# A hybrid encoder layer on one core: DeltaNet's inverse in 64x64 tiles, a convolution spread over two rounds, and the experts' products in four column tiles of 32 tokens

## The reference, cut to what matters

```python
# DeltaNet: short convolution, then a chunked delta rule; each chunk solves a
# unit lower triangular system A (here with chunks of 128 tokens)
qkv = silu(centred_depthwise_conv(qkv, conv_w))       # 5 taps
L = where(strict, einsum('bnhid,bnhjd->bnhij', kb, k) * decay, 0.0)
sol = triangular_solve(L + eye, rhs, lower=True, unit_diagonal=True)
# experts: 16, each takes its C = 2*T/16 best tokens (32 prompt + 64 sample = 96)
gates, idx = top_k(softmax(xt @ w_router).T, C)
xe = xt[idx]
h = silu(xe @ w_gate[e]) * (xe @ w_up[e])             # 2048 -> 1024
ye = (h @ w_down[e]) * gates                          # 1024 -> 2048
out = zeros_like(xt).at[idx].add(ye)
```

## Time and profile before

| | us |
|---|---|
| median of 3 runs | 3360.66 (3359.61 to 3364.0) |
| the profiled execution's own time | 3364.69 |
| its span in the trace | 3362.9 |
| DeltaNet, about | 624 to 1640 |
| output projection and routing, about | 1640 to 1990 |
| experts | 1990 to the end |

### The profile page before, as it was taken

How to read it: one execution, slowest core, us unless ns; L and a number is a source line. 1 busy time by engine, 2 the same in 40 slices (tenths; PEclk the granted TensorE clock), 3 DMA queues, 4 the chain that set the end, 5 groups by cost and what they waited for, 6 DMA issues and landing times. The chain is left out here.

```text
span 3362.9 us, 28930 instructions
## 1 busy us (share of the span) xinstructions
PE 3262.4 (97%) x11412; PEld 1742.5 (52%) x11412; DVE 889.7 (26%) x1519; ACT 517.8 (15%) x1349; POOL 381.8 (11%) x400
## 2 busy tenths in 40 slices
PE   8999999999999999989999989999999999999998
PEld 4544555567867767757544643333333333333333
DVE  2001454326546547567301230000000000000000
ACT  4101554122132132041100110000000000000000
POOL 0000100032141141152000000000000000000000
PEclk9999999999999999989999889999999999999999
DMA  4111100211111111040421378888888888888884
GB/s 168 50 67 59 38 26 19 83 51 51 47 35 51 48 35 51 23 150 14 159 104 50 126 281 318 316 317 316 317 316 316 317 316 317 316 317 317 317 308 142
DMA packets 165417, 560.59 MB, mean 167 GB/s; under 512 B 11888, under 2 KB 44488, under 8 KB 143304
## 3 DMA queue, kind: packets, MB, share of 16 engines
q1 hardware_dynamic: 161223, 534.07, 44.0%
q0 software_dynamic: 4096, 25.17, 3.4%
HBM read 524.25 MB, written 34.96 MB: 166 GB/s over the span
## 5 line engine op out<-in xcount | busy, mean ns | idle before, releaser
L2360 PE MATMUL psum<-wbuf,xeT 128*96 128x512 f32 x1040 | 454.1, 595 | 2.1 <-ACT h L2411 1.4
L2360 PE MATMUL psum<-xT,xeT 128*96 128x512 f32 x1008 | 437.6, 592 | 0.0
L1219 PE MATMUL psum<-xT,wbuf 128*128 128x512 f32 x720 | 330.6, 594 | 0.3 <-PEq L611 0.3
L2360 PEld LDWEIGHTS psum<-wbuf,xeT 128*96 128x96 f32 x1040 | 170.1, 164 | 280.0 <-issue 279.0
L2360 PEld LDWEIGHTS psum<-xT,xeT 128*96 128x96 f32 x1008 | 164.3, 163 | 268.3 <-issue 268.3
L1963 PE MATMUL psum<-wbuf,xT 128*128 128x512 f32 x656 | 289.9, 604 | 1.0 <-PEq L1144 1.0
L459 PE MATMUL psum<-wbuf,xT 128*128 128x512 f32 (+1 forms) x704 | 281.1, 559 | 0.9 <-DVE xT L379 0.9
L2378 PE MATMUL psum<-xT,hT 128*96 128x512 f32 x528 | 229.3, 592 | 0.7 <-ACT hT L2406 0.7
L2436 DVE COPY hT<-psum 128x384 f32<-128x384 f32 x16 | 8.9, 557 | 822.6 <-PE psum L2342 822.6
L2378 PE MATMUL psum<-wbuf,hT 128*96 128x512 f32 x496 | 215.5, 592 | 0.7 <-DVE hT L2436 0.7
L1963 PEld LDWEIGHTS psum<-wbuf,xT 128*128 128x128 f32 x656 | 127.1, 195 | 158.7 <-issue 158.7
(11 more groups left out here) (297 smaller groups left out, 3045.4 us busy)
## 6 DMA issues: line engine op xcount, KB each, us to landing
wbuf<-in_w_up SPq DMA_DIRECT2D x47, 2048.0 KB, 9.3
xT<-in_w_gate SPq DMA_DIRECT2D x46, 2048.0 KB, 7.2
xT<-in_w_down SPq DMA_DIRECT2D x33, 2048.0 KB, 9.8
wbuf<-in_w_down SPq DMA_DIRECT2D x31, 2048.0 KB, 8.0
wbuf<-in_w_gate SPq DMA_DIRECT2D x18, 2048.0 KB, 7.3
xT<-in_w_up SPq DMA_DIRECT2D x17, 2048.0 KB, 11.6
wbuf<-in_w_in SPq DMA_DIRECT2D x14, 2048.0 KB, 8.8
wbuf<-in_w_o SPq DMA_DIRECT2D x6, 4096.0 KB, 14.7
```

The source lines that it names most:

```text
L1219: last = nc.tensor.matmul(ps[:, b, 0:SS_], wg[:, m % 2, d, h * P:(h + 1) * P], k.xT[:, d, SP_:T], start=(d == 0), stop=(d == KD - 1))
L2360: last = nc.tensor.matmul(ps[0:CT, 2 * (u // 4) + half, :], xeT[:, q, :], m[:, kk, 512 * half:512 * half + 512], start=(q == 0), stop=(q = ...
```

## The change: what it does, and the diff

In `deltanet`: (1) at levels 1 to 5 `product` and `update` compute only the two 64x64 diagonal blocks, each with a product of its own on rows and columns 0 to 63 or 64 to 127 of the array; `advance` becomes two instructions, one for each block. (2) Of head 1's five taps, two stay behind round 0 and three move to levels 1 to 3 of round 1. (3) The sums of squares come later within the next pair's first projection; those of the last pair move into the projection before it, the last pair's ScalarE order is changed to suit, and its transposes of k come ahead of `gram`.

In `moe`: (4) the 96 tokens are split into G = 3 groups of 32 and the output columns into J = 4 quarters. A product has 32 tokens as stationary columns and writes 32 partitions of PSUM; four products, one for each quarter of the columns, go to the four column tiles of the array: 3 x 4 products where there were 4 of `up` (or 32 x 3 where there were 32 of `down`), each 512 columns long. (5) A unit of weights holds two rows of gate and of up together, or two full row blocks of down; it is loaded by two DMAs of 1 MB in pieces of 8 KB. `up` waits for VectorE's multiply of the expert before, where its gate half waited for SiLU alone. (6) The hidden layer and the result now lie as 4 quarters x 32 tokens on 128 partitions: SiLU and multiply are one instruction each, the hidden layer is transposed by six 128x128 transposes instead of eight, the result is scaled by three instructions after the last unit of `down`. (7) The scatter is three DMAs of 128 quarter rows of 2 KB, and the row numbers and gates are spread over the partitions once, at the start of the stage, by five small VectorE instructions, six transposes and two copies; the routing stage loses a transpose and a copy.

```diff
+                def blockwise(x, n, left, right, lv):
+                    for lo, hi in ((0, P),) if lv == LV else ((0, P // 2), (P // 2, P)):
+                        last = nc.tensor.matmul(ps[lo:hi, x, n * P + lo:n * P + hi], left[lo:hi, x, n, lo:hi], right[lo:hi, x, n, lo:hi],
+                                                start=True, stop=True)
+                    return last
                 def product(i, r, x, lv):
                     pe.wait_ge(s_t[x], i * 18 + 6 * r + lv)
                     if r == 0 and lv == 1:
                         pe.wait_ge(s_kvc, i * 6 + 3)
                     for n in range(4):
-                        last = nc.tensor.matmul(ps[:, x, n * P:(n + 1) * P], lt[:, x, n], tinv[:, x, n], start=True, stop=True)
+                        last = blockwise(x, n, lt, tinv, lv)
                     last.then_inc(s_m1[x], 1)
                 def update(i, r, x, lv):
                     pe.wait_ge(s_p1[x], i * 18 + 6 * r + lv)
                     for n in range(4):
-                        last = nc.tensor.matmul(ps[:, x, n * P:(n + 1) * P], p1[:, x, n], tt[:, x, n], start=True, stop=True)
+                        last = blockwise(x, n, p1, tt, lv)
...
-                        project(i + 1, 0, between={2: lambda: sum_squares(i, 0), 3: lambda: sum_squares(i, 1),
-                                                   6: lambda: sum_squares(i, 2), 8: lambda: sum_squares(i, 3)})
-                        project(i + 1, 1, between={0: lambda: gram(i, 0), 8: lambda: k_transposes(i)})
+                        project(i + 1, 0, between={6: lambda: sum_squares(i, 0), 7: lambda: sum_squares(i, 1),
+                                                   11: lambda: sum_squares(i, 2), 13: lambda: sum_squares(i, 3)})
+                        project(i + 1, 1, between={4: lambda: gram(i, 0), 10: lambda: k_transposes(i)})
                     else:
-                        for n in range(4):
-                            sum_squares(i, n)
+                        k_transposes(i)
...
+                        steps = {6: lambda: output(i)}
+                        if i + 2 == HP:
+                            steps.update({14: lambda: sum_squares(i + 1, 0), 15: lambda: sum_squares(i + 1, 1),
+                                          26: lambda: sum_squares(i + 1, 2), 31: lambda: sum_squares(i + 1, 3)})
+                        project(i + 1, 5, between=steps)
...
-                    copy_tile(i, 5)
+                    if more:
+                        copy_tile(i, 5)
                     square(i, 2)
-                    square(i, 3)
+                    if more:
+                        square(i, 3)
                     act.preload_act_table_set(TABLES)
-                    for n in range(4):
-                        rms(i, n)
+                    rms(i, 0)
+                    if not more:
+                        square(i, 3)
+                    rms(i, 1)
+                    if not more:
+                        copy_tile(i, 5)
+                    rms(i, 2)
+                    rms(i, 3)
...
-                    flat = tt[:, x].rearrange("p n c -> p (n c)")
-                    nc.vector.tensor_tensor(flat, flat, ps[:, x, :], ALU.subtract).then_inc(s_tt[x], 1)
+                    bank = ps[:, x, :].rearrange("p (n c) -> p n c", n=4)
+                    for lo, hi in ((0, P),) if lv == LV else ((0, P // 2), (P // 2, P)):
+                        o = tt[lo:hi, x, :, lo:hi]
+                        last = nc.vector.tensor_tensor(o, o, bank[lo:hi, :, lo:hi], ALU.subtract)
+                    last.then_inc(s_tt[x], 1)
...
+                            if r == 1 and lv <= 3 and more:
+                                convolve(i + 1, 1, [lv + 1])
...
-                            convolve(i + 1, 1)
+                            convolve(i + 1, 1, range(2))
...
+    G, J = CT // 32, 4
+    XBANK = (3, 4, 6, 7)
...
+        h = sb("h", [P, G, FF // J])
         hT = sb("hT", [P, FF // P, CT])
-        ye = sb("ye", [CT, D])
-        gate = sb("gate", [CT, 1])
-        ss = sb("scatter_sample", [CS, 1], U32)
-        sp = sb("scatter_prompt", [CP, 1], U32)
+        ye = sb("ye", [P, G, D // J])
+        gate = sb("gate", [P, G])
+        gates = sb("gates", [P, G, NE])
+        quarter = sb("quarter_rows", [P, G, NE], U32)
+        sq = sb("scatter_rows", [P, G], U32)
+        rep = sb("replicated", [NE, 2, G, J, 32])
...
+                        for x, d in enumerate((gate_d, up_d)):
+                            src = d[bass.ds(ex, 1), :, 2 * u:2 * u + 2, :].rearrange("o p k f -> (o p) (k f)")
+                            sync.dma_start(ring[w % RING][:, 2 * FF * x:2 * FF * x + 2 * FF], src).then_inc(s_w[w % RING], 16)
...
-                        src = down_d[bass.ds(ex, 1), :, :, 512 * q:512 * q + 512].rearrange("o p k f -> (o p) k f")
-                        sync.dma_start(ring[w % RING].rearrange("p (k n) -> p k n", k=8), src).then_inc(s_w[w % RING], 16)
+                        for x in range(2):
+                            src = down_d[bass.ds(ex, 1), :, 2 * q + x, :].rearrange("o p n -> (o p) n")
+                            sync.dma_start(ring[w % RING][:, D * x:D * x + D], src).then_inc(s_w[w % RING], 16)
...
-                        for j in range(4):
-                            f = 4 * b + j
-                            last = nc.tensor.transpose(ps[:, 6 + b, j * CT:(j + 1) * CT], h[:, f * P:(f + 1) * P], k.ident[0:CT, 0:CT])
+                        for g in range(G):
+                            last = nc.tensor.transpose(ps[:, 6 + b, g * P:(g + 1) * P], h[:, g, b * P:(b + 1) * P], k.ident)
...
-                                pe.wait_ge(s_sg, ex)
-                        if u == 4 and w0:
-                            pe.wait_ge(s_h, ex)
+                                pe.wait_ge(s_h, ex)
                         pe.wait_ge(s_w[w % RING], loaded(e, w))
-                        m = ring[w % RING].rearrange("p (k f) -> p k f", k=4)
-                        for kk in range(4):
-                            q = 4 * (u % 4) + kk
-                            for half in range(2):
-                                last = nc.tensor.matmul(ps[0:CT, 2 * (u // 4) + half, :], xeT[:, q, :], m[:, kk, 512 * half:512 * half + 512],
-                                                        start=(q == 0), stop=(q == KD - 1))
+                        m = ring[w % RING].rearrange("p (x k f) -> p x k f", x=2, k=2)
+                        for kk in range(2):
+                            q = 2 * u + kk
+                            for g in range(G):
+                                for j in range(J):
+                                    last = nc.tensor.matmul(ps[32 * j:32 * j + 32, g, :].rearrange("p (x n) -> p x n", x=2),
+                                                            xeT[:, q, 32 * g:32 * g + 32], m[:, :, kk, 256 * j:256 * j + 256],
+                                                            start=(q == 0), stop=(q == KD - 1))
                         last.then_inc(s_u, 1)
                 def down(ex, e, w0, more):
                     pe.wait_ge(s_ha, ex + 1)
                     pe.wait_ge(s_hd, ex + 1)
-                    for q in range(4):
-                        w = w0 + q
-                        if q < 2 and more:
-                            pe.wait_ge((s_xa, s_xd)[q], ex * 2 + 5)
-                        elif q < 2:
-                            pe.wait_ge(s_ye, ex * 4 + 4)
-                        else:
-                            pe.wait_ge(s_ye, ex * 4 + q + 3)
+                    for u in range(4):
+                        w = w0 + u
                         pe.wait_ge(s_w[w % RING], loaded(e, w))
-                        m = ring[w % RING].rearrange("p (k n) -> p k n", k=8)
-                        for f in range(8):
-                            last = nc.tensor.matmul(ps[0:CT, 4 + q % 2, :], hT[:, f, :], m[:, f, :], start=(f == 0), stop=(f == 7))
+                        m = ring[w % RING].rearrange("p (k n) -> p k n", k=2)
+                        for kk in range(2):
+                            f = 2 * u + kk
+                            for g in range(G):
+                                if f == 0 and more and g < 2:
+                                    pe.wait_ge((s_xa, s_xd)[g], ex * 2 + 5)
+                                elif f == 0 and not more:
+                                    pe.wait_ge(s_ye, ex * G + g + 1)
+                                for j in range(J):
+                                    last = nc.tensor.matmul(ps[32 * j:32 * j + 32, 3 + g, :], hT[:, f, 32 * g:32 * g + 32],
+                                                            m[:, kk, 512 * j:512 * j + 512], start=(f == 0), stop=(f == 7))
...
+                pe.wait_ge(s_gc, 1)
+                for which in range(2):
+                    for g in range(G):
+                        last = nc.tensor.transpose(ps[:, 0, (which * G + g) * NE:(which * G + g + 1) * NE],
```

(28 more changed lines are left out.)

81 lines of the change are left out of this document (42 added, 39 removed).

## The result

| | before | after |
|---|---|---|
| median of the runs shown, us | 3360.66 | 3074.22 (3 runs, 3072.95 to 3075.09) |
| ratio to before, 95% interval | | 0.9144 [0.9126, 0.9161] |
| span of the profiled execution, us | 3362.9 | 3071.2 |
| first product of the inverse (line 1289) starts | 774.7 | 771.7 |
| last `product` instruction of the inverse starts | 1612.4 | 1591.5 |

Forecast were 3063 us, with a range of 2995 to 3235 and 0.85 for faster. The measured time is 11 us above the forecast and inside the range. By stages, the experts gave 271.6 us (1373.0 to 1101.4; 258 forecast) and DeltaNet about 18 (837.7 us from the first to the last `product` instruction of the inverse, then 819.8; 40 forecast). The remaining 3 us lie ahead of DeltaNet, where nothing was changed.

The account below looks back on a forecast made before the run. TensorE was taken as the bound, by the columns it streams, with DMA next. From the profiled 3364.7 us, less 258 (experts) and 40 (DeltaNet), came 3067, or 3063 as that execution was 4.0 above the median; range 2995 to 3235.

Parts of the forecast that it names:

- The round of four: Experts' `up` and `down`: four column tiles stream at once, 0.429 us a round, 61.8 us an expert in 144 rounds.
- rival B: Experts' products: a column tile's loads cannot run beside other tiles' products; 0.821 us a round, about 3894 us; chance 9%.
- C: Experts' products: tiles go one after the other, 1.716 us a round, 249 us an expert, near 6000 us; chance 5%.
- TensorE's floor: Experts' stage: TensorE's time for products and transposes, 63.8 us an expert.
- The DMA limit: Experts' stage: DMA becomes the limit; 25 us at 359 GB/s, the rest at 417, 1.5 us added: 69 us an expert.
- Rival A: Experts' stage: full DMA queues hold 343 GB/s throughout, 77.8 us an expert, about 3203 us in all; chance 16%.
- The stage: Experts' stage as a whole: 16 x 69 us with start, loads ahead and tail, 1115 us for 1373, -258 us.
- the last unit behind its landing: End of the experts' stage: 5 us added for the last unit of weights behind its landing.
- Levels: DeltaNet levels 1 to 5: 64x64 blocks take 0.5 us off each of 60 levels, -30 us.
- The halves: DeltaNet's `advance` in two instructions: 2 x 0.412 for 0.675 us, +0.3 us a level for both x.
- The spread convolution: DeltaNet, three pairs: TensorE's 2.30 us wait goes, -7 us; taps in round 1 charged 5; net -2 us.
- The last pair's start: DeltaNet's last pair: sums and first two norms within the projection take 8 us off the 26.0 us start.

Follow-up runs that it names:

- Half the bytes: Changed kernel with each DMA of weights in the experts' stage bringing half its bytes, stale data in the rest, every product kept: 3028.04 us, ratio 0.9004.
- no scatter: Changed kernel without the three accumulating DMAs of each expert and the wait for them, outputs lacking the experts' part: 3017.1 us, ratio 0.897.
- the kernel with full tiles: Changed kernel with 128x128 products and one whole subtraction at all levels of DeltaNet's inverse: 3081.98 us, ratio 0.9164.
- The run with one subtraction: Changed kernel with small products but the subtraction whole, level 1's update staying in full tiles: 3049.89 us, ratio 0.9071.

## Why the prediction was right, and where it was not

**The round of four.** Forecast 0.429 us if all lies side by side; measured 0.429 (four starts within 0.02 us, loads of 0.110 us beside them). Rivals B and C are out. TensorE's floor was forecast at 63.8 us and is 64.06; the transposes take 2.13 us (0.81 + 1.32) for 2.0. The Trainium skill's rule ("TensorE: Matmul & The Clock Gate", Part 3: Packing small matmuls) that a load overlaps only with a different row group, which stood with rival B, is not what this trace shows: loads for four tiles that share all rows are hidden. The same section's speedup of 2.38 is for three tiles, which no run here has. Carried over to four it would make an expert some 80 us, an estimate; this trace has 0.429/0.107 = 4.0 for four tiles.

**The DMA limit.** Forecast 69 us an expert with TensorE waiting some 5 us; measured 68.2 from about 2220 us on, 4.1 of it waiting. The stretches that the sum rested on the earlier trace rows, 417 and 359 or 343 GB/s, came back as 419 and 343. That the sum came out is partly luck, though. The 25 us at 359 GB/s hold a gather alone and no scatter: their queue moved 0.79 MB, one time 96 rows of 8 KB, and the scatter's DMAs were issued at 2140.11 and 2141.88 us. With the 40 us that hold both, 13.7 MB at 343 GB/s, and the rest at 417 the same sum gives 71 us. The other way went the size of the pieces, which the sum had at nothing. In the kernel before, where only the weights of `down` were coming, in pieces of 2 KB, full engines brought 375 GB/s:

```profile
2165.00:2180.00 15.00, 15.00 (x37) 5.68 (x36) 0.00 (x0) 0.00 (x0) 0.00 (x0) 1.00 1.04 375
```

The changed kernel, with all pieces of 8 KB, has 422 GB/s at a share of 1.01 between 2250 and 2280 us. For the 8.4 MB of `down` that is 8.4/0.375 - 8.4/0.422 = 2.5 us an expert, an estimate; no run changes the pieces alone. Half the bytes, or no scatter, take the limit away, which shows it as the cause. Rival A (343 GB/s throughout) is out: 383 GB/s over the stage, 385 forecast. (The range's upper end, said to be rival A with a DeltaNet that gains nothing, would be 3203 + 40 = 3243 us and not 3235; nothing hangs on it.) The 358 GB/s of the Trainium skill ("DMA: Bandwidth & Descriptors", Specifications) would have given 74.6 us, an estimate; the trace has 393 GB/s over 1000 us. The figure stands there as half of what an HBM gives its two cores, and here one core ran, so it was the wrong bound for this case.

**The stage.** Forecast 1115 us, measured 1101.4, 13.6 less. By the terms: an expert at 68.2 for 69 us makes -12.8. The 5 us "for the last unit behind its landing" had no row, and the last `down` runs its 20.84 us without a wait: -5. Start (1969.8 to the first product at 1975.7) and tail (3071.2 - 3053.4 = 17.8 us, forecast 17.5) together +1.2. From the first product to the last, 1077.7 us are 16 x 68.2 less 13.5, so the units loaded ahead gave 13.5 where 17 stood: +3.5. The 1.5 us for smaller scatter rows were too much: the queue takes 7.0 for 6.6 us an expert.

**Levels: the step that failed.** "I take -0.5 us" a level, -30 us; measured -0.07 us in the level shown, and 8 us in all with the tiles taken back. The -0.9 of two groups of small products was right in kind: by the starts, -0.36 at the update (1.09 to 0.73) and -0.39 at the product of x = 1 (1.00, read in the kernel with full tiles, to 0.61). The halves were charged +0.3 from a 256-column row of another instruction; they cost +0.48 (2.81 to 3.29 us). The price of one half was right (0.418 us for 0.412); by the starts the two pairs add 0.38 us, and the step from the transpose to the next subtraction adds 0.10 (0.74 for 0.64). And the projection step between small products became 0.19 us longer (0.86 to 1.05), which the sum did not have: -0.36 - 0.39 + 0.48 + 0.19 = -0.08. The run with one subtraction confirms the halves' part: 0.47 us a level come back. The forecast sign that VectorE would be over 90% busy in rounds was wrong, too: between 985 and 1215 us it is busy for 139.30 of 230 us, since it still waits for TensorE's products in each level.

**The spread convolution.** -2 forecast, about -5 measured. The gap of 2.30 us went (0.33 is left), and if the 5 us are right, the 11 us of taps in round 1 cost less than the 5 charged; VectorE was busy for only 61% of the stretch above.

**The last pair's start.** -8 forecast, and nothing came. The first part of the reasoning held: 26.0 us to the first product became 1455.96 - 1440.0 = 16.0, for 18 forecast. The sentence "what is late next is `lower`" was half of it: TensorE does wait 4.81 us for VectorE ahead of the product of x = 1, but behind that stood the weights w_o (4.74 us), issued when the projection ends, which the move itself made later. The forecast had not followed what the sums' new place does to the projection's end, and who waits for that.

Together DeltaNet is -17, of which -8 (tiles) and some -5 (taps, near the noise) have a run each and the rest is not told apart (the sums of the other pairs were moved too, and no run takes that back), where -30, -2 and -8 stood. It gave 23 us less than forecast and the experts' stage 14 more: that the total is within 0.4% is owed in part to two errors of opposite sign. The 3 us ahead of DeltaNet and the place of the two profiled executions (4.0 us above the median before, 1.3 below it after) make up the small rest.

## What to carry to other kernels

When an operation is cut in blocks to make one engine shorter, count what the cut does to the engine behind it in the chain: here a pair of half subtractions cost 0.85 us for 0.69 and gave back 24 of the 32 us that 64x64 products had won, while the subtraction could stay whole once one full update had left zeros in the bank. Here, products with 96 stationary columns became three quarters as long by four column tiles, and then the limit to work out was that of the DMA engines, per stretch with and without gathers and scatters, and by the size of the pieces. Before work is moved ahead of an event, look up what is issued at that event, since it comes later by the same amount.

## What the runs showed that was not expected

Products of different column tiles need not start in program order: with three in a row on one tile, TensorE still kept three of four tiles busy (0.154 us an instruction for 0.108), and products of the following loop started among those of the one before. So the order in which products name their tiles cost 0.046 us an instruction, and not the three to four times that I had expected from a strict order.

The step of the projection between `product` and `update` takes 1.05 us where its 128x128 products stand between 64x64 ones, and 0.86 where all are 128x128. That the change of tile size costs these 0.2 us is the likely reading; no run takes it alone. The same code of DeltaNet took 819.8 to 823.6 us in different programs with nothing else changed in the stage; what does that wasn't tried.
